# Value projections by halves of the rows: 96 matmuls of 512 columns for 192 of 256 in each pair of slabs

## The reference, cut to what matters

```python
def retention_mixer(h, w_in, w_out):
    rq, rk, rv, rg = _split(h @ w_in, RET_SPLITS)          # 1024, 1024, 2048, 2048 columns
    q = rotary(_heads(rq, 4), pos)
    k = rotary(_heads(rk, 4), pos) * 256 ** -0.5
    v = _heads(rv, 4)                                      # 4 heads of 512 columns
    o = retention_chunkwise(q, k, v)                       # o_t = sum_{s<=t} gamma^(t-s) (q_t . k_s) v_s
    o = rms_norm(o) * silu(_heads(rg, 4))
    return _merge(o) @ w_out

# even layer of the second block: vm, vd = 512 columns each of h @ w_in (moba, differential)
# odd layer of the second block:  vc = 512 columns of h @ w_in (dilated)
```

## Time and profile before

| | |
|---|---|
| median of 3 runs | 2916.53 us (2906.45 to 2918.85) |
| span of the profiled execution | 2912.0 us |
| PE busy | 2796.6 us, 96% |
| PEld (weight loads) busy | 2244.8 us, 77% |
| DVE, ACT, POOL busy | 48%, 33%, 18% |
| chain that ended last | PE 88%, DVE 5%, ACT 4% |
| DMA | 296.36 MB, mean 102 GB/s |

### The profile page before, as it was taken

The page is one execution under the profiler, slowest core; times in us unless marked ns, Lnnn a source line. Parts: engine busy times, 40 slices in busy tenths (PEclk is TensorE's granted clock), DMA queues, the critical chain, the costliest instruction groups (busy, mean ns, idle before and its releaser), DMA issues.

```text
span 2912.0 us, 33354 instructions
## 1 busy us (share of the span) xinstructions
PE 2796.6 (96%) x13978; PEld 2244.8 (77%) x13978; DVE 1410.5 (48%) x2076; ACT 964.0 (33%) x1278; POOL 533.2 (18%) x414
## 2 busy tenths in 40 slices
PE   7998989999999999999999999899999998999998
PEld 4776657888887888888888877688888875788886
DVE  6645546666544333373222455555345365454453
ACT  3435444322233322243222333432223244332222
POOL 2563301100112201221001100012012100021121
PEclk9999989999999999999999999999999999999999
DMA  6322103456332222222632322122322311222321
GB/s 240 123 88 92 54 8 145 174 183 222 139 100 92 91 85 79 76 87 100 172 116 70 119 81 81 40 101 86 108 101 74 115 58 66 73 93 76 114 83 69
DMA packets 51093, 296.36 MB, mean 102 GB/s; under 512 B 6617, under 2 KB 6745, under 8 KB 25088
## 3 DMA queue, kind: packets, MB, share of 16 engines
q1 hardware_dynamic: 44912, 276.58, 27.1%
q0 software_dynamic: 4736, 15.34, 2.0%
q10 hardware_dynamic: 1296, 2.32, 0.2%
HBM read 283.46 MB, written 8.65 MB: 100 GB/s over the span
## 4 chain that ended last, share of the span: by engine, by line
PE 88%; DVE 5%; ACT 4%; issue 1%; POOL 1%; DMA 0%; SPq 0%; DVEq 0%
PE ps L218 88%; DVE wlo L211 1%; PE ps L1312 1%; ACT whi L200 1%; DMA F<-in_ada 0%; ACT F L1329 0%; DVE F L412 0%; DVE hl L416 0%; DVE ada L460 0%; DVE F L2260 0%; ACT L253 0%; ACT E L2833 0%; DVE F L827 0%; ACT E L2831 0%; ACT hh L430 0%
## 5 line engine op out<-in xcount | busy, mean ns | idle before, releaser
L218 PE MATMUL ps<-hh,whi 128*128 128x512 f32 x2088 | 829.6, 397 | 12.4 <-ACT F L2811 5.8
L218 PE MATMUL ps<-hl,whi 128*128 128x512 f32 x2088 | 815.4, 391 | 0.0
L218 PE MATMUL ps<-hh,wlo 128*128 128x512 f32 x2088 | 814.6, 390 | 0.0
L211 DVE TENSOR_TENSOR wlo<-raw,whi 128x2048 fp32r<-128x2048 f32 (+2 forms) x235 | 497.3, 2116 | 509.3 <-ACT whi L200 509.2
L218 PE MATMUL ps<-R,whi 128*128 128x512 f32 x2080 | 650.0, 391 | 8.0 <-DVE wlo L211 3.1
L200 ACT ACTIVATE whi<-raw 128x2048 fp32r<-128x2048 f32 (+2 forms) x235 | 409.6, 1743 | 686.2 <-PE ps L218 681.7
L218 PEld LDWEIGHTS ps<-hh,whi 128*128 128x128 f32 x2088 | 393.1, 188 | 103.7 <-issue 12.2
L218 PEld LDWEIGHTS ps<-R,whi 128*128 128x128 f32 x2080 | 390.5, 188 | 95.3 <-issue 6.9
L218 PEld LDWEIGHTS ps<-hl,whi 128*128 128x128 f32 x2088 | 393.0, 188 | 83.2
L218 PEld LDWEIGHTS ps<-hh,wlo 128*128 128x128 f32 x2088 | 393.4, 188 | 82.2 <-issue 3.3
L218 PE MATMUL ps<-R,wlo 128*128 128x512 f32 x1040 | 404.7, 389 | 0.0
(11 more groups left out here) (343 smaller groups left out, 2587.5 us busy)
## 6 DMA issues: line engine op xcount, KB each, us to landing
F<-in_ada SPq DMA_DIRECT2D x32, 1024.0 KB, 4.9
raw<-in_fs0in SPq DMA_DIRECT2D x22, 1024.0 KB, 6.1
raw<-in_fs1in SPq DMA_DIRECT2D x22, 1024.0 KB, 4.8
raw<-in_fc0in SPq DMA_DIRECT2D x22, 1024.0 KB, 4.9
raw<-in_fc1in SPq DMA_DIRECT2D x22, 1024.0 KB, 4.8
Rf<-in_ada0h SPq DMA_DIRECT2D x24, 512.0 KB, 3.5
raw<-in_fs0out SPq DMA_DIRECT2D x16, 704.0 KB, 4.5
raw<-in_fs1out SPq DMA_DIRECT2D x16, 704.0 KB, 4.1
```

The costliest lines, as they stand in the source:

```text
L211: e.tensor_tensor(m.wlo[n % 2][:, 0:size], m.raw[m.slot[n]][:, 0:size], m.whi[n % 2][:, 0:size].bitcast(F32), SUB).then_inc(*s.up("wlo", n))
L218: return e.matmul(out, l, r, start=start, stop=stop, skip_group_check=True)
```

## The change

A pair of value slabs is cut the other way: slab 0 holds rows 0 to 511 by all 512 columns, slab 1 rows 512 to 1023 by the same columns (`half_slabs`; a slab stays 128 x 2048). `pe_tok_half` takes the place of `pe_tok` in the four stages: for each quarter of the tokens 4 row blocks x 3 matmuls of 512 columns; the first slab begins the sum in a whole bank and leaves it open, the second ends it. So the quarters are copied once, 512 wide, after the second slab; the copies after the first are gone, and so are TensorE's waits for them. In retention the banks 4 to 7 hold the open sums, so the scores go to banks 0 to 3, and `dve_ret` masks them from there; the second slab no longer waits for the masking; the wait for each copy moves from ahead of values times scores to ahead of the matmul that reads it. `pe_tok` stays for the hybrid stage.

```diff
-KC = {"mluq": 2, "mlukv": 1, **{...}}
+KC = {"mluq": 2, "mlukv": 1, "retv": 4, "mbv": 4, "dfv": 4, "dlv": 4, **{...}}
+def pe_tok_half(e, s, m, n, half, banks, free):
+    s.wait_ge("wlo", n)
+    hi, lo = m.w(n)
+    for t in range(4):
+        if half == 0:
+            free(t)
+        for k in range(4):
+            h = [a[:, t * P:(t + 1) * P] for a in m.h(4 * half + k)]
+            i = mm3_left(e, m.ps[banks[t]][:, :], *h, hi[:, k, :], lo[:, k, :], half == 0 and k == 0, half == 1 and k == 3)
+        i.then_inc(*s.up("tile", n, t))
+    s.also("tile", n, "all")
 def pe_ret(e, s, m):
-            def free(t):
-                if j:
-                    s.wait_ge("a", h, t)
-                elif h == 2:
+        def v_free(t):
+            if h == 2:
...
-        run(pe_tok(e, s, m, m.at["retv", 2 * h], (4, 5, 6, 7), v_free(0)))
+        pe_tok_half(e, s, m, m.at["retv", 2 * h], 0, (4, 5, 6, 7), v_free)
         s.wait_ge("rot", h, 3)
         s.wait_ge("rot_mul", h, 1, 3)
         for c in range(4):
-            s.wait_ge(V_BY[c % 2], "ret", h, 0, c)
             for n in range(2):
-                t = mm(e, m.ps[4 + c][:, 0:T - c * P], ...)
+                t = mm(e, m.ps[c][:, 0:T - c * P], ...)
-        run(pe_tok(e, s, m, m.at["retv", 2 * h + 1], (4, 5, 6, 7), v_free(1)))
+        pe_tok_half(e, s, m, m.at["retv", 2 * h + 1], 1, (4, 5, 6, 7), v_free)
-        for c in range(4):
-            s.wait_ge(V_BY[c % 2], "ret", h, 1, c)
         for d in range(4):
             for c in range(4):
                 s.wait_ge("a", h, c)
+                s.wait_ge(V_BY[c % 2], "ret", h, c)
                 t = mm(e, m.ps[d][:, c * P:], v[:, c, d * P:(d + 1) * P], m.f(R_AS[c], T - c * P), c == 0, c == 3)
 def act_ret(e, s, m):      # dve_ret alike, t in (0, 2)
-            if h and j == 0:
+            if h and j == 1:
                 s.wait_ge("pv", h - 1, 3)
-            for t in (1, 3):
+            for t in (1, 3) if j else ():
                 s.wait_ge("tile", n, t)
-                e.activation(v[:, t, 256 * j:256 * j + 256], m.ps[4 + t][:, 0:256], ACT.Copy)
+                e.activation(v[:, t, :], m.ps[4 + t][:, :], ACT.Copy)
 def dve_ret(e, s, m):
-                    e.tensor_tensor(m.f(R_AS[c], T - c * P), m.ps[4 + c][:, 0:T - c * P], m.f(R_DM, T - c * P), MUL)
+                    e.tensor_tensor(m.f(R_AS[c], T - c * P), m.ps[c][:, 0:T - c * P], m.f(R_DM, T - c * P), MUL)
 def pe_h64(e, s, m, st):
-            def free(t):
-                if i:
-                    s.wait_ge(V_BY[t % 2], st, 0, t)
-            run(pe_tok(e, s, m, m.at[v, i], TOK_BANKS, free))
+            pe_tok_half(e, s, m, m.at[v, i], i, TOK_BANKS, lambda t: None)
 def act_tok(e, s, m, st, n, j, values):      # dve_tok alike, t in (0, 2)
-    for t in (1, 3):
+    for t in (1, 3) if j else ():
-        e.activation(values[:, t, 256 * j:256 * j + 256], m.ps[TOK_BANKS[t]][:, 0:256], ACT.Copy, scale=...)
+        e.activation(values[:, t, :], m.ps[TOK_BANKS[t]][:, :], ACT.Copy, scale=...)
 def pe_diff(e, s, m):
             def free(t):
-                if i:
-                    s.wait_ge(V_BY[t % 2], "diff", 0, t)
-                elif t == 0:
+                if t == 0:
                     s.wait_ge("o_lo_dve", "even", 3)
-            run(pe_tok(e, s, m, m.at["dfv", i], TOK_BANKS, free))
+            pe_tok_half(e, s, m, m.at["dfv", i], i, TOK_BANKS, free)
+def half_slabs(W, order):
+    return np.concatenate([slabs(W[512 * n:512 * n + 512], [o], 512) for o in order for n in range(2)])
-    o["retv"] = slabs(w, run(2048, 256, 2048), 256)
+    o["retv"] = half_slabs(w, run(2048, 512, 2048))
...
```

More of the change, by code:

```diff
@@ L171, in w @@
         return cut(self.whi), cut(self.wlo)
-KC = {"mluq": 2, "mlukv": 1, **{f"{t}{l}out": 11 for t in ("fs", "fc") for l in range(2)}}
+KC = {"mluq": 2, "mlukv": 1, "retv": 4, "mbv": 4, "dfv": 4, "dlv": 4, **{f"{t}{l}out": 11 for t in ("fs", "fc") for l in range(2)}}
 def sp_slab(e, s, m, n):
@@ L1016, in pe_ret @@
             run(pe_tiles(e, s, m, qk[n], (b, b + 1), m.h, ready))
-        def v_free(j):
-            def free(t):
-                if j:
-                    s.wait_ge("a", h, t)
-                elif h == 2:
[L1023 to L1028, removed]
-        run(pe_tok(e, s, m, m.at["retv", 2 * h], (4, 5, 6, 7), v_free(0)))
+        def v_free(t):
+            if h == 2:
+                s.wait_ge("x", "ret", "half", 4 + t)
+            elif h and t:
+                s.wait_ge("g", "ret", 4 * h - 4 + t)
+            elif h:
+                s.wait_ge("rs_o", "ret", h - 1)
+        pe_tok_half(e, s, m, m.at["retv", 2 * h], 0, (4, 5, 6, 7), v_free)
         s.wait_ge("rot", h, 3)
@@ L1071, in act_ret @@
             v = m.f(R_V, 2048).rearrange("p (c n) -> p c n", c=4)
-            if h and j == 0:
+            if h and j == 1:
                 s.wait_ge("pv", h - 1, 3)
-            for t in (1, 3):
+            for t in (1, 3) if j else ():
                 s.wait_ge("tile", n, t)
-                e.activation(v[:, t, 256 * j:256 * j + 256], m.ps[4 + t][:, 0:256], ACT.Copy).then_inc(*s.up("v_act", "ret", h, j, t))
+                e.activation(v[:, t, :], m.ps[4 + t][:, :], ACT.Copy).then_inc(*s.up("v_act", "ret", h, t))
         act_slab(e, s, m, m.at["retg", 2 * h] + 1)
@@ L1151, in dve_ret @@
             dve_slab(e, s, m, n + 1)
-            if h and j == 0:
+            if h and j == 1:
                 s.wait_ge("pv", h - 1, 3)
-            for t in (0, 2):
+            for t in (0, 2) if j else ():
                 s.wait_ge("tile", n, t)
-                e.tensor_copy(v[:, t, 256 * j:256 * j + 256], m.ps[4 + t][:, 0:256]).then_inc(*s.up("v_dve", "ret", h, j, t))
+                e.tensor_copy(v[:, t, :], m.ps[4 + t][:, :]).then_inc(*s.up("v_dve", "ret", h, t))
             if j == 0:
@@ L1423, in pe_h64 @@
                 for t in range(4):
-                    s.wait_ge(V_BY[t % 2], st, 1, t)
+                    s.wait_ge(V_BY[t % 2], st, t)
             else:
@@ L1465, in act_tok @@
 def act_tok(e, s, m, st, n, j, values):
-    for t in (1, 3):
+    for t in (1, 3) if j else ():
         s.wait_ge("tile", n, t)
-        e.activation(values[:, t, 256 * j:256 * j + 256], m.ps[TOK_BANKS[t]][:, 0:256], ACT.Copy, scale=m.acol[:, 12 + t:13 + t]).then_inc(*s.up("v_act", st, j, t))
+        e.activation(values[:, t, :], m.ps[TOK_BANKS[t]][:, :], ACT.Copy, scale=m.acol[:, 12 + t:13 + t]).then_inc(*s.up("v_act", st, t))
 def dve_tok(e, s, m, st, n, j, values):
-    for t in (0, 2):
+    for t in (0, 2) if j else ():
         s.wait_ge("tile", n, t)
-        e.tensor_scalar(values[:, t, 256 * j:256 * j + 256], m.ps[TOK_BANKS[t]][:, 0:256], m.acol[:, 12 + t:13 + t], None, MUL).then_inc(*s.up("v_dve", st, j, t))
+        e.tensor_scalar(values[:, t, :], m.ps[TOK_BANKS[t]][:, :], m.acol[:, 12 + t:13 + t], None, MUL).then_inc(*s.up("v_dve", st, t))
 def dve_qk(e, s, m, st, p, n, a):
@@ L1588, in pe_diff @@
                 for t in range(4):
-                    s.wait_ge(V_BY[t % 2], "diff", 1, t)
+                    s.wait_ge(V_BY[t % 2], "diff", t)
             else:
@@ L3303, in layout @@
     o["mbqk"] = slabs(w, [two(128 * p, 512 + 128 * p) for p in range(4)], 256)
-    o["mbv"] = slabs(w, run(512, 256, 1024), 256)
+    o["mbv"] = half_slabs(w, run(512, 512, 1024))
     o["dfqk"] = slabs(w, [two(1536 + 128 * p, 2048 + 128 * p) for p in range(4)], 256)
-    o["dfv"] = slabs(w, run(512, 256, 2560), 256)
+    o["dfv"] = half_slabs(w, run(512, 512, 2560))
     o["eveno"] = slabs(a["even_w_out_2"][0], run(1024, 256), 256)
@@ L3309, in layout @@
     o["dlqk"] = slabs(w, [two(128 * p, 512 + 128 * p) for p in range(4)], 256)
-    o["dlv"] = slabs(w, run(512, 256, 1024), 256)
+    o["dlv"] = half_slabs(w, run(512, 512, 1024))
     o["mlq"] = slabs(w, [r(1536, 1792)], 256)
```

4 lines of the change are left out of this document (2 added, 2 removed).

## The result

The changed kernel takes **2903.89 us** (median of 6 runs, 2900.39 to 2906.7) against 2916.24 us before (6 runs). The ratio is **0.9962**, 95% interval 0.995 to 0.9974: 11.1 us by the ratio, between 7.6 and 14.6 (the medians are 12.35 us apart). In a second set of executions of both kernels it came out at 0.9968 (0.9957 to 0.998). Predicted was 10.3 us, 2906.2.

The account below looks back on a forecast made before the run. PE, busy for 96% of the span, was taken to bound the kernel. Matmul savings of 4.15 and 3.92 us plus 2.88 for a wait, less 0.64 for wider copies, made 10.3 us: 2906.2 us, range 2895 to 2916.

Parts of the forecast that it names:

- The price of a matmul: Value slabs: 1344 matmuls of 256 columns at 119.9 ns become 672 of 512 at 227.1 ns; bounds 213 and 239.8.
- Slabs of retention and the three stages: Shorter value slabs save 4.15 us in retention and 3.92 us in the even, differential and odd stages.
- Head 0: Retention's head 0: first slab saves nothing, its wait for POOL's rotation grows from 2.0 to 2.6 us; second saves 0.58.
- Heads 1 to 3: Retention: the rotation ends 5.2 us before the scores, so a first slab 0.6 us shorter costs no wait.
- The wait before values times scores: Retention, four heads: PE's wait for ACT's last copy becomes hidden, saving 4 x 0.72 = 2.88 us; bounds 0 and 2.88.
- The wait before the first scores: Even, differential and odd stages: the wider scaled copy takes 0.21 us more each, -0.64 us; joint 0.93 to 1.25 us.
- Sum: Whole kernel: 4.15 + 3.92 + 2.88 - 0.64 = 10.3 us saved, giving 2906.2 us.
- The cheap 512-column matmul: Rival for the value slabs: one 512-column matmul costs far less than two of 256; 120 us gained, 2796 us; chance 2%.
- the dear one: Rival: the wide form with weights moving has its own price; slower from 243 ns per matmul, 2931 us at 265; chance 4%.
- The gain that doesn't arrive: Rival: waits absorb first-slab savings as at head 0; 3.6 us remain, 2913 us, or in part 2910; chance 11%.
- The clock did fall elsewhere: Rival: low-clock stretches shift; both vanish, 4.8 us more gained, 2901 us, chance 12%; new ones appear, 2909 us, 9%.
- The rule against the row: Skill's isolated gap would give some 4 us in total, its 131 ns per matmul 43 us; the prediction kept the trace's rows.

Follow-up runs that it names:

- The late conversion: Changed kernel with VectorE converting retention's second value slab only after the rotation's last step by POOL: 2906.19 us, one run.
- the 384-and-128 form: Changed kernel with each 512-column matmul of the value slabs issued as one of 384 and one of 128 columns: 2942.93 us, one run.

## Why the prediction was right, point by point

- **The price of a matmul.** Right: 226.9 ns where 227.1 was taken, in the middle of bounds (213 to 239.8) that had been left wide for want of a row. Cutting the matmuls in two gave back 11.51 us per slab, and 7.9 of the 10.5 us by stages. The mean durations would have promised 120 us; the windows over a counted stretch gave the right price before anything was built.
- **Slabs of retention and the three stages.** First slabs 11.51 to 10.89 (0.61 expected, 0.62 found), second ones 11.59 to 11.02 (0.58, 0.57). Pairs 23.11 to 21.89, 1.22 where 1.31 was taken: the slow start of the first matmuls behind the sums was not counted.
- **Head 0.** Right: its first slab is shorter and nothing came of it, the joint went from 2.12 to 2.85 us (2.7 was forecast). The late conversion shows the cause, and that 2 us more lay there.
- **Heads 1 to 3.** Right: no wait for the rotation.
- **The wait before values times scores.** 4 x 0.72 expected; with the waits alone moved, 4 x 0.80, of which 0.08 is a quicker start of the fp32 matmuls. The copy stayed hidden, as forecast: the joint is 0.23 us in all four heads and the matmuls behind it wait for nothing. This term was under-sized by the 0.08, 0.3 us in all.
- **The wait before the first scores.** 0.93 to 1.25 us, as worked out; the copy is 0.69 us, as worked out from the rows of two others.
- **Sum.** 7.03 expected in retention, 7.44 found; 3 x 1.10 in the others, 3 x 1.01 found: 10.3 and 10.5 us. The mechanism is shown by these stages. The times alone could not have told as much: 11.1 us (7.6 to 14.6) and, the second time, 9.3 hold both, and that they came within 1 us of 10.3 is luck.
- **The rivals.** The cheap 512-column matmul and the dear one are out by the pace. The gain that doesn't arrive was real at head 0 alone. The clock did fall elsewhere: the odd stage's stretch went (-1.36), one came in the latent attention (+1.6), and the differential stage kept its 10.24 us in two pieces. It cancels here. The changed kernel's second profile spent 3.0 us more between the differential and the odd stage, with 6.8 us more at 0.50. So where the stretches fall differs between two executions of one kernel, and they were rightly given to the range and not to the forecast.
- **The rule against the row.** The Trainium skill's isolated gap of columns/2.4 + 2.5 ns and its 131 ns at 512 columns (both in "TensorE: Matmul & The Clock Gate", as the prediction cites them) were weighed against some 13 ns and 227 ns from the trace. The kernels cut in pieces stand with the trace: some 13 ns over the columns at 256 and 512, and no 512-column matmul at 131.

## What to carry to other kernels

Price a matmul by the length of a long, gapless stretch over its count, never by mean durations: here the difference between the two readings was 10 us against 120. Joining two matmuls of 256 columns into one of 512 saves one fixed 13 ns, 75 of them for a microsecond, so a copy that is waited for in full (1.1 us, four times: 4.49 us) weighs as much as some 340 joins: move each wait to the instruction that needs the data. A wait that an engine's neighbour causes, like POOL's addition beside VectorE's conversion, is found by the same instruction taking 1.3 us in one place and 3.2 in another.

## What the runs showed of the hardware that was not expected

- A matmul of 128 columns in fp32r, each with its own load of weights, comes every 111.4 ns, one of 256 every 119.9, one of 512 every 226.9. Three of 384 and then three of 128 take 859 ns together: the short one behind a long one passes in 60 ns, but the sum is no smaller for it.
- With nothing but 128-column matmuls for 79 to 82 us, PE and PEld busy throughout, the granted clock was 0.50 in three stages almost from start to end (213 ns a matmul, so the floor of 111.4 went with the clock), while the same form in retention, in runs of 21.4 us between fp32 scores, kept 1.00. With the 384-and-128 form the clock held in the same places, but for one stretch of 3.4 us. What decides it is open.
- In code that the change doesn't touch, the start of head 0's first value slab ranged from 891.85 to 903.96 us between profiles, with 44 to 68 us at the lower clock ahead of it: 12.1 us later for 23.9 us more at 0.50. That is 0.4% of the time, as much as the whole change, and sets what a comparison of single runs is worth.
